# Three chunks of expert weights lent a place outside the ring, and all four sums opened before the gather

## The reference

```
h = rms_norm(x, attn_norm_g);  proj = h @ w_in          # q, k, v of two kinds of heads, q of memory heads, gates
x = x + merged(neighbourhood, dilated and memory attention, gated) @ w_out
h = rms_norm(x, ffn_norm_g)
top_val, top_idx = top_k(h @ router_w + router_b, 4);  top_w = softmax(top_val)
for each of 32 experts e, on the tokens that chose it:
    gu = h[tokens] @ w_gu[e] + b_gu[e]
    g, u = min(gu[:, :1024], 7), clip(gu[:, 1024:], -7, 7)
    y = ((u + 1) * g * sigmoid(1.702 * g)) @ w_dn[e] + b_dn[e]
    x[tokens] += y * top_w
out = rms_norm(x, final_norm_g)
```

## Time and profile before

| what | value |
|---|---|
| median of 3 runs | 1239.45 us (1239.34 to 1240.58) |
| profiled execution | 1241.22 us, its span 1239.4 us |
| PE busy | 1182.7 us, 95% |
| DVE, ACT, POOL busy | 269.3, 255.8, 207.3 us |
| DMA | 456.40 MB, mean 368 GB/s |

### The profile page before, as it was taken

One profiled execution on the slowest core, in us unless ns is written; L12 is line 12 of the kernel. 1 busy time (PEld: TensorE's weight loads), 2 busy tenths in 40 slices (PEclk: granted clock), 3 DMA queues, 4 the chain that ended last, 5 costly groups with the idle time before them and its releaser, 6 DMA issues.

```text
span 1239.4 us, 14318 instructions
## 1 busy us (share of the span) xinstructions
PE 1182.7 (95%) x6239; PEld 611.0 (49%) x6239; DVE 269.3 (22%) x539; ACT 255.8 (21%) x531; POOL 207.3 (17%) x89
## 2 busy tenths in 40 slices
PE   8999999999999999999999999999999989999996
PEld 8989877899533343333333333333333333333332
DVE  4147253232421111211111111121111111111112
ACT  6456455334310101101010010010001000000001
POOL 5865755687100000000000000000000000000000
PEclk9999999999999999999999999999999999999999
DMA  9754443499799999999999999999999999999995
GB/s 311 249 159 158 161 159 119 132 352 404 277 416 435 429 429 430 427 431 427 430 429 429 430 434 429 433 425 432 430 430 432 427 434 423 432 429 430 428 426 235
DMA packets 61255, 456.40 MB, mean 368 GB/s; under 512 B 5145, under 2 KB 33593, under 8 KB 43272
## 3 DMA queue, kind: packets, MB, share of 16 engines
q1 hardware_dynamic: 61192, 455.47, 89.3%
HBM read 454.39 MB, written 1.07 MB: 367 GB/s over the span
## 4 chain that ended last, share of the span: by engine, by line
PE 59%; DMA 37%; DVE 1%; ACT 1%; issue 1%; POOL 0%; SPq 0%; DVEq 0%; POOLq 0%; ACTq 0%
PE ps L540 58%; DMA arena<-in_expert_w_gate_up 33%; DMA arena<-in_expert_w_down 3%; PE ps L832 1%; DMA arena<-in_w_mem_kv 1%; ACT arena L1022 0%; POOL w_parts L529 0%; PE ps L826 0%; DVE x_normed L1468 0%; DVE neg_max L1308 0%; ACT w_parts_odd L1002 0%; PE ps L646 0%; PE ps L547 0%; PE ps L623 0%; DVE arena L1297 0%
## 5 line engine op out<-in xcount | busy, mean ns | idle before, releaser
L540 PE MATMUL ps<-arena,gathered_T 128*64 128x512 f32 x2048 | 473.7, 611 | 39.1 <-DMA arena<-in_expert_w_gate_up 39.1
L540 PE MATMUL ps<-arena 128*64 128x512 f32 (+6 forms) x1666 | 342.4, 537 | 2.8 <-DMA arena<-in_expert_w_down 1.3
L540 PEld LDWEIGHTS ps<-arena,gathered_T 128*64 128x64 f32 x2048 | 145.5, 140 | 307.3 <-issue 270.2
L540 PEld LDWEIGHTS ps<-arena 128*64 128x64 f32 (+3 forms) x1666 | 135.8, 154 | 199.4 <-issue 193.0
L529 POOL TENSOR_TENSOR w_parts<-arena,w_parts 128x1024 fp32r<-128x1024 f32 x42 | 102.9, 2472 | 50.5 <-ACT w_parts L1002 40.8
L529 POOL TENSOR_TENSOR w_parts_odd<-arena,w_parts_odd 128x1024 fp32r<-128x1024 f32 x38 | 90.9, 2413 | 49.4 <-ACT w_parts_odd L1002 49.4
L1412 DVE TENSOR_SCALAR arena<-arena 128x128 f32<-128x128 f32 x64 | 19.3, 343 | 317.8 <-PE ps L826 317.8
L1143 ACT COPY arena<-ps 128x256 f32<-128x256 f32 x32 | 11.9, 372 | 361.2 <-PE ps L826 361.2
L1418 DVE TENSOR_SCALAR arena<-ps 128x512 f32<-128x512 f32 x32 | 22.1, 691 | 274.4 <-PE ps L540 274.4
L1134 ACT ACTIVATE gathered_T<-ps,g_cols 128x128 f32<-128x128 f32 x128 | 36.5, 368 | 171.4 <-PE ps L540 171.4
L540 PEld LDWEIGHTS ps<-arena,x_normed 128*128 128x128 f32 x512 | 59.5, 191 | 24.8 <-issue 24.3
(11 more groups left out here) (178 smaller groups left out, 729.8 us busy)
## 6 DMA issues: line engine op xcount, KB each, us to landing
arena<-in_expert_w_gate_up SPq DMA_DIRECT2D x54, 4096.0 KB, 39.4
arena<-in_expert_w_down SPq DMA_DIRECT2D x62, 2048.0 KB, 39.7
arena<-in_expert_w_gate_up SPq DMA_DIRECT2D x20, 2048.0 KB, 13.0
arena<-in_w_in SPq DMA_DIRECT2D x29, 1024.0 KB, 5.3
arena<-in_w_out SPq DMA_DIRECT2D x4, 1024.0 KB, 11.5
arena<-in_expert_w_down SPq DMA_DIRECT2D x4, 1024.0 KB, 41.0
arena<-in_w_mem_kv SPq DMA_DIRECT2D x3, 1024.0 KB, 12.1
arena<-t_scratch SPq DMA_DIRECT2D x6, 384.0 KB, 3.7
```

Of the source, the lines that this page charges most:

```text
L540: return nc.tensor.matmul(out, lhsT, rhs, start=start, stop=stop, **kw)
```

## The change

Three chunks get places outside the ring (`LENT`): chunk 6 lies over the second half of `gathered_T` and over `bias_raw`; chunk 7 in the work area over `gate_c`, `up_c`, `sig` and `y_sb`, which are first written after the use of chunk 7 (for this the areas of the mixture of experts are put in another order); chunk 20 in `x`. Each has a semaphore of its own (`lent_in`) and a wait that says when its place is free: chunk 7 after the router's product, chunk 20 after both normed halves of x are written and all four sums are opened, chunk 6 after `bias_ready`. All other chunks move up in the ring (`place_of`), so the ring holds 20 others, and the refills begin at chunk 23. A refill now waits for the chunk that lies in its last slot (`refilled`), and a transfer that would cross the end of the ring is split in two. The small loads into x follow the first refill that waits for chunk 20 or a later one. The router's, ranks' and counts' products move from bank 7 to bank 0, and the sum (1, 1) is opened ahead of the router's second product. In expert 0 the gather comes behind the seventh chunk instead of the sixth, since it leads to writes over chunk 6.

```
+LENT = (6, 7, 20)
-EARLY_AFTER = {36: 0, 38: 4, 39: 6, 40: 8, 41: 10}
-FIRST_LAP = {2: 38, 12: 38, 14: 40, 18: 41, 16: NF}
+EARLY_AFTER = {36: 0, 38: 4, 39: 8, 40: 10, 41: 12}
+FIRST_LAP = {2: 38, 14: 38, 16: 40, 21: 41, 18: NF}
+def place_of(c):
+    return c - sum(lent < c for lent in LENT)
+def ring_slot(c):
+    return (place_of(c) + SCORE_SLOT) % RING
+def refilled(c):
+    return next(b for b in range(c) if b not in LENT and place_of(b) == place_of(c) - RING)
...
-    order = [(0, *t) for t in short]
+    order = [(0, *t) for t in short[:3] + [(6, 1), (7, 1)]]
     for n in range(1, EXPERTS):
-        order += [(n, *t) for t in (long if FIRST_LONG <= n < EXPERTS - 1 else short)]
+        gate_up = [(0, 1), (1, 2), (3, 2), (5, 3)] if n == 2 else long if FIRST_LONG <= n < EXPERTS - 1 else short
+        order += [(n, *t) for t in gate_up]
...
     for e, j, m in order:
-        out[c] = (e, j, m)
+        to_end = min(m, RING - ring_slot(c))
+        out[c] = (e, j, to_end)
+        if to_end < m:
+            out[c + to_end] = (e, j + to_end, m - to_end)
         c += m
...
+            sp.wait_ge(router_ps, 1)
+            load_weights(*TRANSFERS[7], None, 7)
+            sp.wait_ge(normed, 3)
+            sp.wait_ge(tile_normed, 1)
+            sp.wait_ge(sums_open, 1)
+            load_weights(*TRANSFERS[20], None, 20)
+            sp.wait_ge(bias_ready, 1)
+            load_weights(*TRANSFERS[6], None, 6)
+            x_free = False
             for c, (_, _, m) in TRANSFERS.items():
-                if c < RING:
+                if c in LENT or place_of(c) < RING:
                     continue
-                sp.wait_ge(chunk_used, NF + c - RING + m)
+                last_used = refilled(c + m - 1)
+                sp.wait_ge(chunk_used, NF + last_used + 1)
                 load_weights(*TRANSFERS[c], ring_slot(c))
-                if c == RING + 4:
+                if last_used >= 20 and not x_free:
+                    x_free = True
...
+            open_with_x(1, 1)
             pe.wait_ge(parts_in, 1)
             for tt in range(T):
-                last = mm(ps[:, 7, 128 + tt * EXPERTS:128 + (tt + 1) * EXPERTS], router_parts[:, tt * P:(tt + 1) * P], stack4[:],
+                last = mm(ps[:, 0, 128 + tt * EXPERTS:128 + (tt + 1) * EXPERTS], router_parts[:, tt * P:(tt + 1) * P], stack4[:],
                           True, True)
             last.then_inc(router_ps, 1)
...
-            open_with_x(1, 0)
+            open_with_x(1, 0).then_inc(sums_open, 1)
...
                             bias_rows(0, False)
-                            open_with_x(1, 1)
...
-                    if k == 5 and n + 2 < EXPERTS:
+                    if k == (5 if n else 6) and n + 2 < EXPERTS:
```

More of the change, by code:

```diff
@@ L310, in build @@
         landed = [sem(f"landed{i}") for i in range(RING)]
+        lent_in = {c: sem(f"lent_in{c}") for c in LENT}
+        sums_open = sem("sums_open")
         first_in, t5_in_done, consts_in = sem("first_in"), sem("t5_in_done"), sem("consts_in")
@@ L358, in front_landed, with chunk_tile @@
             eng.wait_ge(landed[i % FRONT_RING], 16 * (i // FRONT_RING + 1))
-        def ring_slot(c):
-            return (c + SCORE_SLOT) % RING
+        lent_tile = {6: chunk_at_XT[:], 7: chunk_in_work, 20: x[:].rearrange("p t c -> p (t c)")}
+        def chunk_tile(c):
+            return lent_tile[c] if c in LENT else ring[:, ring_slot(c), :]
         def front_fills(r):
@@ L368, in fills_through @@
         def fills_through(c):
-            return front_fills(ring_slot(c)) + sum(ring_slot(b) == ring_slot(c) for b in TRANSFERS if b <= c)
+            return front_fills(ring_slot(c)) + sum(ring_slot(b) == ring_slot(c) for b in TRANSFERS if b <= c and b not in LENT)
         ALL_CHUNKS = EXPERTS * EXPERT_CHUNKS
         def overflow_fills(j):
-            return front_fills(ring_slot(j)) + sum(ring_slot(c) == ring_slot(j) for c in TRANSFERS) + 1
+            return front_fills(j) + sum(ring_slot(c) == j for c in TRANSFERS if c not in LENT) + 1
         def by_row(dst, tt):
@@ L410, in _, with load_weights @@
         def _(sp):
-            def load_weights(e, j, m, r):
+            def load_weights(e, j, m, r, lent=None):
                 if j < KC:
@@ L417, in load_weights @@
                     src = w_dn[bass.ds(e, 1), :, (j - KC) // 2, first:first + m * CHUNK].rearrange("o p c -> (o p) c")
-                sp.dma_start(ring[:, r:r + m, :].rearrange("p r c -> p (r c)"), src).then_inc(landed[r], 16)
+                if lent is not None:
+                    sp.dma_start(lent_tile[lent], src).then_inc(lent_in[lent], 16)
+                else:
+                    sp.dma_start(ring[:, r:r + m, :].rearrange("p r c -> p (r c)"), src).then_inc(landed[r], 16)
             for tt in range(T):
@@ L812, in bias_rows, with gate_up @@
                     mm(ps[:, b, :], pick[:, pick_slot, :], bias_parts[:, b, :], first, False, skip_group_check=True)
-            def gate_up(slot, k, xt, first=False):
+            def gate_up(weights, k, xt, first=False):
                 for b in range(2):
@@ L818, in gate_up @@
                         last = mm(ps[64 * h:64 * h + 64, b, :], xt[:, k, :],
-                                  ring[:, slot, b * D + 512 * h:b * D + 512 * (h + 1)], first, k == KC - 1,
+                                  weights[:, b * D + 512 * h:b * D + 512 * (h + 1)], first, k == KC - 1,
                                   skip_group_check=True)
@@ L833, in turn_act, with down @@
                 last.then_inc(aT_ps, 1)
-            def down(slot, j, bank):
+            def down(weights, j, bank):
                 for kk in range(2):
@@ L840, in down @@
                         last = mm(ps[64 * hn:64 * hn + 64, bank, :], aT[:, k % 4, BLK * (k // 4):BLK * (k // 4) + BLK],
-                                  ring[:, slot, kk * D + 512 * hn:kk * D + 512 * (hn + 1)],
+                                  weights[:, kk * D + 512 * hn:kk * D + 512 * (hn + 1)],
                                   k == 0, k == KC - 1)
@@ L860, in weights_landed @@
             def weights_landed(c):
-                pe.wait_ge(landed[ring_slot(c)], 16 * fills_through(c))
+                if c in LENT:
+                    pe.wait_ge(lent_in[c], 16)
+                else:
+                    pe.wait_ge(landed[ring_slot(c)], 16 * fills_through(c))
             def down_products(n, bank):
@@ L870, in down_products @@
                         weights_landed(c)
-                    down(ring_slot(c), j, bank)
+                    down(chunk_tile(c), j, bank)
             for n in range(EXPERTS):
@@ L949, in _ @@
                             if k % 2 == 0:
-                                pe.wait_ge(landed[ring_slot(k)], (b + overflow_fills(k)) * 16)
-                            gate_up(ring_slot(k), k, XT[:, 0, :, 0:BLK])
+                                pe.wait_ge(landed[k], (b + overflow_fills(k)) * 16)
+                            gate_up(ring[:, k, :], k, XT[:, 0, :, 0:BLK])
                             if k == 3:
@@ L961, in _ @@
                             if j % 2 == 0:
-                                pe.wait_ge(landed[ring_slot(j)], (b + overflow_fills(j)) * 16)
-                            down(ring_slot(j), j, 3)
+                                pe.wait_ge(landed[j], (b + overflow_fills(j)) * 16)
+                            down(ring[:, j, :], j, 3)
             pe.wait_ge(y_ready, EXPERTS)
```

39 lines of the change are left out of this document (21 added, 18 removed).

## The result

The changed kernel takes 1241.97 us, median of 22 runs (1239.49 to 1244.36), against 1239.45 us for the kernel before (22 runs, 1238.99 to 1241.62). The medians are 2.5 us apart; the ratio is 1.0017 (95% interval 1.0010 to 1.0023), which is 2.1 us. The forecast was 1236.6 us, 2.8 us faster, with a range of 1234.6 to 1239.3, so the time lies outside it, on the other side. The profiled execution took 1241.20 us with a span of 1239.4 us, both as before.

A forecast was written before the change was run, and what follows sets the result against it. DMA was taken to bound the kernel from 611.68 us on. Of a filled 7.1 us hole 3.5 us were kept, less 0.7 for more transfers: 2.8 us off the 1239.45 us median, so 1236.6 us, range 1234.6 to 1239.3.

The forecast's parts named there:

- Step 1: Sum (1, 1) opened ahead of the router's second product: all that hangs on the router comes 0.45 us later.
- Step 2: The same opening leaves the first expert, where it took 1.0 us: PE is 0.5 us earlier from the fifth chunk on.
- Step 3: Loads of chunks 7, 20 and 6 keep the DMA queue busy until 330.2 us; PE waits for none.
- Step 4: Gather of experts 2-3 moved behind chunk 6: the same 2.0 us of PE one chunk later, costing nothing.
- Step 5: First refills run dry twice, once empty for 3.8 us; chunks 28-29 land at 353.6, 42-43 at 390.1 us.
- Step 6: First four-chunk refill, 44-47, waits for chunk 27's use, capping the gain: landing at 400.35 against 403.85, 3.5 us kept.
- Step 7: From chunk 44 on, 17 more transfers from splits at the ring's end, at 0.04 us each: 0.7 us lost.
- nearly all is given back: Rival: refills into the empty queue cost up to 1.8 us more, splits up to 0.12 each; 1238.8 us, chance 0.29.
- Slower: Rival: the 17 added transfers, where DMA is the bound, cost 1.1 us each; 15.2 us slower, 1254.6 us, chance 0.05.
- All is kept: Rival: the wait for chunk 27 does not bind; 7.1 us less 0.7 is gained, 1233.0 us, chance 0.06.
- What I said would show the mechanism: Signs: full DMA 324-330 us, gaps near 336 and 344-347, PE's first weight wait after 611, at least 429 GB/s in 600-1200.
- chance of 0.58 for faster: Stated as 0.57, from 0.45 of the forecast's case, 0.07 of nearly all is given back, 0.06 of All is kept.

The follow-up runs named there:

- half a pass: Kernel before with the sum (1, 1) opened ahead of the router's second product, and GpSimd's pass over x cut to half its columns; 1239.60 us, ratio 0.9998.
- second profile: The changed kernel run again with no edit, as a control against the kernel before; 1242.03 us, ratio 1.0009.
- The splits alone: Kernel before, nothing lent, its transfers from chunk 44 on cut in two as in the changed kernel (135 instead of 118); 1240.76 us, ratio 1.0004.
- the early opening alone: Kernel before, nothing lent, with sum (1, 1) opened ahead of the router's second product and router and rank products in bank 0; 1240.08 us, ratio 1.0004.
- the one with 25-27 cut: Changed kernel with the refill of chunks 25-27 cut into 25-26 and 27; 1242.57 us, ratio 1.0023.
- the last opening behind the gather: Changed kernel with sum (1, 1) opened behind the gather instead of ahead of the router's second product, chunk 6 loaded before 20; 1242.19 us, ratio 1.0012.
- twos for one expert more: Changed kernel with transfers of four chunks starting at expert 5 instead of 4, so chunks 44 to 51 go by twos; 1240.94 us, ratio 1.0006.

## Why the prediction was wrong

The forecast was a gain of 2.8 us; measured is a loss of 2.5 by the medians, 1.8 and 3.2 by the two profiles counted from R. By the first profile the forecast missed by 4.6 us: 2.7 up to the landing of 44-47 (R + 88.1 instead of 85.4), 1.9 behind it (838.2 us instead of 836.3).

- **Step 1, mis-sized.** Forecast 0.45 us on all that hangs on the router. Measured 0.27 directly (half a pass), and 0.72 from VectorE's operation that now waits for the end of GpSimd's pass (0.89 less 0.17): 1.0 us. In three of five profiles the clock's low stretch adds another 1.2 to 1.3 us up to the first refill. I looked for what waits for PE and not for what the delayed work would meet on its own engine.
- **Step 2** held as far as the opening is gone from the first expert, but its 1.0 us only cancels the 1.0 us of step 1. PE is not 0.5 us ahead of the kernel before: 44-47, which wait for its use of chunk 27, are issued at R + 74.1, before at R + 73.9.
- **Step 3** held. All three lent loads were in the queue in time, and PE waits for none.
- **Step 4** held; the runs show nothing at that place.
- **Step 5, mis-sized.** The second dry spot is where it was forecast, at 343 to 346 us; of the first, near 336 us, the profile shows only a DMA share of 0.77 in 336 to 337. But 28-29, into the emptied queue, took 7.8 us to land, not 7.1, and the stream from there to 42-43 took 37.4 us, not 36.5. Of this, 0.6 are one late landing (34, a single chunk, 3.1 us behind the one ahead of it and not 2.45; in the second profile 32-33 are 0.8 us late), and the rest is about the two small loads, which take 2.5 us here and not 2.1. With 0.8 us from the later issue (0.6 of it step 1's) that makes 42-43 land 2.4 us later than forecast, counted from R.
- **Step 6.** The gain at 44-47 was 3.5 us in the forecast and is 0.8 in one profile of the changed kernel and -0.5 in the other. The cap that I built it on did not bind, since the queue reached them later than the wait did.
- **Step 7, right in kind and short by a stall.** Forecast 0.7 us for what comes behind 44-47, measured 2.6 and 2.7 in the two profiles. The splits alone cost 1.2. The rest is something the prediction had no term for. In a full queue landings come 2.45 us apart per chunk, except for a few that are 1.1 to 1.7 us late, called stalls here. The kernel before has three, at 551.4, 776.8 and 1007.3 us, 3.8 us in all; the kernel with the splits alone three, 4.2 us; the early opening alone three, 4.7 us, and the same with half the pass; the changed kernel four, at 471.0, 687.1, 922.7 and 1153.3 us, 6.2 us in all; its second profile four, 6.1 us, and the one with 25-27 cut four, 6.3 us. Without them the stream from 44-47 to the last landing takes 818.2 to 819.2 us in these kernels with the old transfers and 819.4 to 820.0 in those with 17 more: 0.2 to 1.8 us, 0.01 to 0.11 each, around the 0.04 that I took. By this account the fourth stall is the rest. It is an account of where the time stands in the profiles, not a test, and other variants do not fit it: with the last opening behind the gather there are eight delays of 0.4 to 0.7 us, 4.0 in all, and yet a stream as long as the changed kernel's (825.5 us); with twos for one expert more there are three, 3.5 us, and the stream without them still takes 821.2.

The last transfer of the changed kernel, from which its stream's 825.6 us are read (it lands at 1190.93 + 35.9 = 1226.8, and 44-47 at 401.2):

```profile
1190.93 4.24 SPq L449 DMA_DIRECT2D arena<-in_expert_w_down  x1
```
```profile
arena<-in_expert_w_down SPq DMA_DIRECT2D x1, 1024.0 KB, 35.9
```

The first of the four in the changed kernel, two transfers issued one behind the other:

```profile
445.26 0.33 SPq L449 DMA_DIRECT2D arena<-in_expert_w_gate_up  x1
...
446.98 0.33 SPq L449 DMA_DIRECT2D arena<-in_expert_w_gate_up  x1
```
```profile
arena<-in_expert_w_gate_up SPq DMA_DIRECT2D x1, 3072.0 KB, 21.7
...
arena<-in_expert_w_gate_up SPq DMA_DIRECT2D x1, 1024.0 KB, 24.0
```

They land at 467.0 and 471.0: 4.0 us for one chunk. Between these two landings stands one of the page's 50 packets of the instruction queue (467 to 469 us):

```profile
q1 hardware_dynamic: 93, 0.89, 107.4%
q8 instruction: 1, 0.02, 3.3%
```

The kernel before has one at 549 to 551 us, right before its first stall. The same holds for every landing of this kind: in ten of the twelve profiles there are 32 that are over 1.0 us late, and each has an instruction packet that began 2.1 to 6.9 us before it, while of all the other landings three in ten have one that near. So the late landings go with these packets, as far as a coincidence in time can show it. But there are 29 of them between 44-47 and the last landing in every profile, one about every 29 us, and most do no harm. If a landing counts only when the slowest of the 16 engines is through, and a packet holds up one engine (3.3% of 16 engines' 2 us is 1.06 us of one), then only each eighth or so falling on the engine that is last anyway would give the 211 to 245 us between stalls; I didn't test it. Whether three or four fall in the run would then depend on which engine is last behind the first refills, which the change altered. That link is argued, not shown.

**The rivals.** Nearest is "nearly all is given back" (1238.8 us), whose mechanism, landings into an empty queue that cost more the second time, is part of step 5's miss; its price was too small, since it knew neither the held operation nor the fourth stall. "Slower" by transfers paid one by one is refuted by the splits alone. "All is kept" is refuted by the landing at R + 88.1. What I said would show the mechanism mostly did: full DMA from 324 to 328 (0.84 in the two microseconds behind), an empty stretch near 344, 429 GB/s. So these signs tell that the hole was filled and not that time was saved. PE's wait for weights begins later, too. PE's first matmuls that waited for a weight, before and then in the changed kernel, and the changed kernel's first long DMA piece in the chain:

```profile
648.81 1.08 PE L540 MATMUL ps<-arena,gathered_T 128*64 128x512 f32 x4 [0.24 <-DMA arena<-in_expert_w_gate_up]
```
```profile
675.86 1.29 PE L582 MATMUL ps<-arena,gathered_T 128*64 128x512 f32 x4 [2.52 <-DMA arena<-in_expert_w_gate_up]
```
```profile
656.07 40.78 DMA arena<-in_expert_w_gate_up
```

The chain enters a DMA at its issue, so the 611.68 of the earlier trace rows and the 656.07 here are issues. The transfer of 611.68 lands at 648.8 us, and PE's first wait is there and not at 611.68. Counted from R the first wait ends at 333.9 us before and at 362.8 now, one expert later, and still no gain. PE closes in on the DMA by only some 2 to 3 us an expert (26.5 to 27.5 us of PE in the chain against 12 x 2.45 = 29.4 of transfers), so a lead that is a microsecond longer moves this point by a transfer or more; it is a poor measure of the end.

One sum of the prediction is off by 0.01: 0.45, 0.07 and 0.06 make a chance of 0.58 for faster, not 0.57.

**What stays open.** Why a small VectorE operation is held in one place of the pass and not 0.27 us earlier; why 28-29 take 7.8 us (7.6 to 8.0 in every profile with lent chunks); why 44-47 land 0.7 us behind the queue's pace; what decides the number of stalls, and what else lengthens the stream in the late-opening variant and in the one with twos. So of the 1.9 us that were missed behind 44-47 some 0.5 are the splits (1.2 instead of 0.7), and the cause of the other 1.4 is not shown. The ten runs leave no version with lent chunks that beats the kernel before: with the early opening gone, fewer cuts, and twos for one more expert the ratio is 1.0003 (0.9994 to 1.0012), and the 7.1 us of filled hole are still not to be seen.

## What to carry to other kernels

Filling an idle stretch of the DMA queue early in a long stream pays only what is still left where the stream turns from bound by the consumer to bound by itself; here 7.1 us of bytes were 0.8 us or less at that point, 1.4 with the opening moved, since the next refills wait for PE and meet an empty queue. When an operation is moved, look at what the delayed dependents will run beside on their own engines and on the neighbour's, not only at the delay. And compare two profiles from a mark behind the part that varies from execution to execution, or 1.8 us of front will pass for a gain.

## What the hardware showed

- A VectorE operation on 128x2 values took 0.17 us, and 0.88 to 0.90 us in five profiles where it began 0.27 us later in a GpSimd pass over 128x1024, ending with that pass.
- After 1.17 to 1.18 us of idle and a few short products PE's granted clock went to 0.5 for 3.4 us in three of five profiles, and in none of the seven with 0.45 to 0.46 us of idle there.
- Each DMA of 1 MB in a queue that is full lands 2.45 us behind the one ahead, as part of a pair or alone; each added transfer brought 144 more packets (63991 less 61255, for 19 transfers) and cost some 0.01 to 0.11 us.
- In a full queue three or four landings of a run are 1.1 to 1.7 us late, 211 to 245 us apart, in nine of the twelve profiles. All of them, and one more in a tenth profile, had an instruction packet that began 2.1 to 6.9 us before, as three in ten of the other landings had.
